# Gate projection of a SwiGLU layer as seven block products instead of eight, in a hand-scheduled decoder kernel

## The reference, cut to what matters

```python
def swiglu(x, w_up, w_down):
    gate, up = jnp.split(x @ w_up, 2, axis=-1)
    return (jax.nn.silu(gate) * up) @ w_down

for i in range(DEPTH):
    ...
    x = x + y
    x = x + swiglu(rms_norm(x, norm_ffn[i]), ffn_w_up[i], ffn_w_down[i])
    gate = jax.nn.sigmoid(x @ ple_w_gate[i] + ple_b_gate[i])
    x = x + gate * (p[i] @ ple_w_proj[i])
```

## Time and profile before

| what | value |
|---|---|
| time, median of 3 runs | 1915.02 us (1914.77 to 1915.72) |
| span of the profiled execution | 1913.6 us |
| PE busy | 1878.2 us, 98% of the span, 13698 matmuls |
| ACT, DVE, POOL busy | 729.3, 742.3, 784.1 us (38%, 39%, 41%) |
| chain that ended last | PE 86%, issue 5%, DVE 3%, POOL, ACT and DMA 2% each |
| matmuls of the shared `job` (L2292) in that chain | 72% of the span |

### The profile page before, as it was taken

The page is one execution under the profiler, slowest core; times in us unless marked ns, Lnnn a source line. Parts: engine busy times, 40 slices in busy tenths (PEclk is TensorE's granted clock), DMA queues, the critical chain, the costliest instruction groups (busy, mean ns, idle before and its releaser), DMA issues.

```text
span 1913.6 us, 35924 instructions
## 1 busy us (share of the span) xinstructions
PE 1878.2 (98%) x13698; PEld 1742.4 (91%) x13698; DVE 742.3 (39%) x871; ACT 729.3 (38%) x1091; POOL 784.1 (41%) x662
## 2 busy tenths in 40 slices
PE   7999999999999999999999999999999999999997
PEld 7999999999999999998555655999999999999997
DVE  6777632111111122697766668222231111111213
ACT  4676733322222234543433343423433322212333
POOL 3333554444554544565110110544535545544541
PEclk9999999999999999999999999999999999999999
DMA  4222232222222222423479678232322222222222
GB/s 128 91 76 84 88 96 73 82 89 83 82 83 81 82 79 77 97 72 99 146 259 312 231 253 297 89 94 70 107 78 82 83 83 82 81 85 83 78 83 78
DMA packets 187278, 210.26 MB, mean 110 GB/s; under 512 B 24483, under 2 KB 150051, under 8 KB 187119
## 3 DMA queue, kind: packets, MB, share of 16 engines
q1 hardware_dynamic: 186946, 208.71, 35.3%
q10 hardware_dynamic: 224, 0.07, 0.0%
HBM read 168.09 MB, written 40.64 MB: 109 GB/s over the span
## 4 chain that ended last, share of the span: by engine, by line
PE 86%; issue 5%; DVE 3%; POOL 2%; ACT 2%; DMA 2%; ACTq 0%; POOLq 0%; SPq 0%; DVEq 0%
PE ps L2292 72%; POOL W_LO L671 2%; PE ps L2677 2%; PE ps L2640 2%; PE ps L2579 2%; PE ps L2618 1%; DMA out_ml_C_s_dram<-C_HALVES 1%; PE ps L2513 1%; PE ps L2628 1%; PE ps L2697 1%; DVE H_PAD L1731 1%; PE ps L2502 0%; PE ps L2573 0%; PE ps L2524 0%; PE ps L2706 0%
## 5 line engine op out<-in xcount | busy, mean ns | idle before, releaser
L671 POOL TENSOR_TENSOR W_LO<-W_RAW,W_HI 128x512 fp32r<-128x512 f32 x464 | 631.1, 1369 | 717.9 <-ACT W_HI L972 651.4
L972 ACT ACTIVATE W_HI<-W_RAW 128x512 fp32r<-128x512 f32 x484 | 299.0, 628 | 709.0 <-PE ps L2292 703.8
L2292 PE MATMUL ps<-A_HI,W_HI 128*128 128x288 f32 x2296 | 493.9, 297 | 8.7 <-DVE A_LO L1567 4.8
L2292 PE MATMUL ps<-A_LO,W_HI 128*128 128x288 f32 x2296 | 492.2, 296 | 0.0
L2292 PE MATMUL ps<-A_HI,W_LO 128*128 128x288 f32 x2296 | 492.0, 296 | 0.0
L2292 PEld LDWEIGHTS ps<-A_HI,W_HI 128*128 128x128 f32 x2296 | 370.2, 189 | 11.3 <-issue 8.8
L2292 PEld LDWEIGHTS ps<-A_HI,W_LO 128*128 128x128 f32 x2296 | 370.4, 189 | 0.0
L2292 PEld LDWEIGHTS ps<-A_LO,W_HI 128*128 128x128 f32 x2296 | 370.4, 189 | 0.0
L1813 DVE TENSOR_TENSOR X<-X,ps 128x1152 f32 (+1 forms) x36 | 48.8, 1354 | 312.4 <-PE ps L2292 312.4
L2292 PE MATMUL ps<-G_HI,W_HI 128*128 128x288 f32 x768 | 164.7, 296 | 0.5 <-DVEq L1839 0.5
L2292 PE MATMUL ps<-G_HI,W_LO 128*128 128x288 f32 x768 | 164.4, 296 | 0.0
(11 more groups left out here) (404 smaller groups left out, 2254.0 us busy)
## 6 DMA issues: line engine op xcount, KB each, us to landing
W_RAW<-in_ffn_w_up_dram SPq DMA_DIRECT2D x176, 256.0 KB, 2.8
C_HALVES<-in_state_mlstm_C_dram SPq DMA_DIRECT2D x64, 512.0 KB, 5.1
out_ml_C_s_dram<-C_HALVES SPq DMA_DIRECT2D x64, 512.0 KB, 5.3
W_RAW<-in_ffn_w_down_dram SPq DMA_DIRECT2D x88, 256.0 KB, 2.6
W_RAW<-in_ml_w_in_dram SPq DMA_DIRECT2D x64, 256.0 KB, 2.8
W_RAW<-in_rg_w_in_dram SPq DMA_DIRECT2D x48, 256.0 KB, 2.8
W_RAW<-in_ple_w_gate_dram SPq DMA_DIRECT2D x32, 256.0 KB, 2.6
W_RAW<-in_ml_w_out_dram SPq DMA_DIRECT2D x32, 256.0 KB, 2.8
```

The source lines that it names most:

```text
L671: pool.tensor_tensor(W_LO[:, s], W_RAW[:, s], W_HI[:, s].bitcast(F32), ALU.subtract).then_inc(lo_ready, 1)
L972: act.activation(W_HI[:, s], W_RAW[:, s], ACT.Copy).then_inc(hi_ready, 1)
L2292: ins = pe.matmul(ps[:, 4 * s + 2 * m + h, 0:HALF_T], a[:, w, k, wc], x[:, h * HALF_T:h * HALF_T + HALF_T], start=i == 0 and k == 0 and q ...
```

## The change

A gate slab is a 2 x 2 block of weights, and the tokens it meets are a 2 x 2 block too (two input chunks, two halves). The product of two 2 x 2 blocks takes eight block products, or seven with the scheme of Winograd and Strassen, if sums and differences of blocks are made first and the seven results are combined afterwards. The change does this for every gate job but the first of each layer (`seven`), 10 of 11 in each layer, so 21 matmuls a slab in place of 24.

- **Weights.** VectorE makes four sums or differences from each pair of raw slabs (`weight_sums`): three go to the new `SUM_RAW`, one overwrites a block of `W_RAW`. ScalarE then rounds the raw slab as before and 384 columns of sums beside it. GpSimd makes the low part of the raw slab, as before, and VectorE that of the sums (`sums_lo`).
- **Tokens.** Four sums of token blocks for each pair of chunks are made once per layer (`scaled_pair` and `sums_hi` on ScalarE, `token_sums` on VectorE), beside the first gate and up jobs, and kept in `B_HI` and `B_LO` (called `T_HI`, `T_LO`), which are free then.
- **Results.** Seven banks hold the products, the eighth is spare; ScalarE copies the first product out, VectorE combines (`combine`). The up job takes the spare bank, the first product's, and two that the first step of combining frees. So TensorE waits for single steps of VectorE.
- The loops of all engines in the channel mixer are written out, and the eight DMAs that store mixer states go ahead of layer 1's mixer instead of behind the kernel's last slabs.

The diff, cut to its core:

```diff
+FORMS = {"11": (0, 0, 0), "12": (0, 1, 0), "22": (0, 1, 1), "s3": (0, 0, 1), "s1": (1, 0, 0), "s2": (1, 1, 0), "s4": (1, 2, 0)}
+PRODUCTS = [("11", "x11"), ("12", "x21"), ("s2", "t2"), ("s3", "t3"), ("s1", "t1"), ("s4", "x22"), ("22", "t4")]
+T_FORMS = ("t1", "t2", "t3", "t4")
...
+def seven(g, j):
+
+    return (g, j) != (0, 0)
...
@@ -964,6 +1028,13 @@
                     return
                 s = phase[0] % 4
                 phase[0] += 1
+                if isinstance(n, int) and n in SUM_SLABS:
+                    raw_t[s].adv()
+                    act.wait_ge(sums_ready, summed.adv() // 2 + 1)
+                    act.wait_ge(slab_used, n - 4 + 2 * RING)
+                    act.activation(W_HI[:, s], W_RAW[:, s], ACT.Copy)
+                    act.activation(SUM_HI[:, s], SUM_RAW[:, s], ACT.Copy).then_inc(hi_ready, 1)
+                    return
                 act.wait_ge(raw_loaded[s], raw_t[s].adv())
                 stand_alone(act)
...
+            def scaled_pair(i, gain):
+
+                for m in range(2):
+                    ins = act.activation(GATED[:, m, :], X[:, 2 * i + m, :], ACT.Copy, scale=VECS1[:, gain + 2 * i + m:gain + 2 * i + m + 1])
+                ins.then_inc(y_scaled, 1)
+
+            def sums_hi(layer, i):
+
+                act.wait_ge(t_raw, 4 * layer + i + 1)
+                act.activation(T_HI[:, 2 * i:2 * i + 2, :], GATE[:, :, :], ACT.Copy).then_inc(t_hi, 1)
+
+            def first_product(layer, g, j):
+
+                q = seven_number(layer, g, j)
+                act.wait_ge(product_done, 4 * q + 1)
+                act.activation(FIRST_PRODUCT[:, :], ps[:, seven_banks(g, j)[0][0], 0:HALF_T], ACT.Copy).then_inc(first_out, 1)
+
+            def ffn(layer, gain, last_out, gh):
                 for g, (g0, gn) in enumerate(GROUPS):
-                    with loop(act, gn // 2, {**split_per(8), jobs: 8, uses[0]: 1, uses[1]: 1, blk: 1}) as j:
+                    for j in range(gn // 2):
                         for k in range(4):
+                            if not seven(g, j):
+                                scaled_pair(k, gain)
+                            elif k == 3:
+                                first_product(layer, g, j)
                             split_hi()
+                            if not seven(g, j):
+                                sums_hi(layer, k)
 
                         b = blk.adv()
-                        act.wait_ge(psum_freed[0], uses[0].adv())
-                        stand_alone(act)
...
+            def token_sums(layer, i):
+
+                dve.wait_ge(y_scaled, 4 * layer + i + 1)
+                x, t = pair4(GATED[:, :, :]), pair4(GATE[:, :, :])
+                link(dve.tensor_tensor(t[:, 0:4:2], x[:, 1:4:2], x[:, 0:2], ALU.subtract))
+                link(dve.tensor_tensor(t[:, 1], x[:, 3], t[:, 0], ALU.subtract))
+                dve.tensor_tensor(t[:, 3], x[:, 2], t[:, 1], ALU.subtract).then_inc(t_raw, 1)
+                dve.wait_ge(t_hi, 4 * layer + i + 1)
+                dve.tensor_tensor(T_LO[:, 2 * i:2 * i + 2, :], GATE[:, :, :], T_HI[:, 2 * i:2 * i + 2, :].bitcast(F32),
+                                  ALU.subtract).then_inc(t_ready, 1)
+                dve.wait_ge(t_ready, 4 * layer + i + 1)
+
+            def weight_sums(layer, g, j, s):
+
+                n = seven_first(layer, g, j)
+                for k in (s, s + 1):
+                    dve.wait_ge(raw_loaded[k], 16 * (n // 4 + 1))
+                w = W_RAW[:, s:s + 2]
+                w11, w21, w12, w22 = w[:, :, 0, 0:P], w[:, :, 0, P:2 * P], w[:, :, 1, 0:P], w[:, :, 1, P:2 * P]
+                s1, s2, s4 = (SUM_RAW[:, s:s + 2, i, :] for i in range(3))
+                link(dve.tensor_tensor(s1, w21, w22, ALU.add))
+                link(dve.tensor_tensor(w21, w11, w21, ALU.subtract))
+                link(dve.tensor_tensor(s2, w22, w21, ALU.subtract))
+                dve.tensor_tensor(s4, w12, s2, ALU.subtract).then_inc(sums_ready, 1)
+
+            def sums_lo(layer, g, j, k):
+
+                dve.wait_ge(hi_ready, seven_first(layer, g, j) + k + 1)
+                dve.tensor_tensor(SUM_LO[:, k], SUM_RAW[:, k], SUM_HI[:, k].bitcast(F32), ALU.subtract).then_inc(lo_dve, 1)
+
+            def combine(layer, g, j):
+
+                q = seven_number(layer, g, j)
+                (_, p2, p6, p7, p5, p3, p4), _ = seven_banks(g, j)
+                c = pair4(GATE[:, :, :])
+                dve.wait_ge(first_out, q + 1)
+                dve.wait_ge(product_done, 4 * q + 2)
+                dve.tensor_tensor(c[:, 0:2], two_banks((p2, p6)), FIRST_PRODUCT[:, :].unsqueeze(1).broadcast_to([P, 2, HALF_T]), ALU.add)\
+                    .then_inc(combined, 1)
+                dve.wait_ge(combined, 4 * q + 1)
+                dve.wait_ge(product_done, 4 * q + 3)
+                dve.tensor_tensor(c[:, 2], ps[:, p7, 0:HALF_T], c[:, 1], ALU.add).then_inc(combined, 1)
+                dve.wait_ge(combined, 4 * q + 2)
+                dve.wait_ge(product_done, 4 * q + 4)
+                dve.tensor_tensor(c[:, 1:4:2], c[:, 1:3], ps[:, p5, 0:HALF_T].unsqueeze(1).broadcast_to([P, 2, HALF_T]), ALU.add)\
+                    .then_inc(combined, 1)
+                dve.wait_ge(combined, 4 * q + 3)
+                dve.wait_ge(slab_used, jobs.adv(4) + 2 * RING)
+                dve.tensor_tensor(c[:, 1:3], c[:, 1:3], two_banks((p3, p4)), ALU.add).then_inc(combined, 1)
+                dve.wait_ge(combined, 4 * q + 4)
+                dve.tensor_tensor(pair5(GATE[:, :, :]), pair5(GATE[:, :, :]), RB, ALU.mult).then_inc(gate_scaled, 1)
...
+            def ahead(layer, g, j, part):
+
+                if part == 0:
+                    weight_sums(layer, g, j, 0)
+                    weight_sums(layer, g, j, 2)
+                    for k in range(3):
+                        sums_lo(layer, g, j, k)
+                else:
+                    sums_lo(layer, g, j, 3)
+
             def ffn(layer, hi, lo):
                 for g, (g0, gn) in enumerate(GROUPS):
-                    with loop(dve, gn // 2, {jobs: 8, uses[0]: 1, uses[1]: 1, blk: 1, ys: 1, step: 1}) as j:
+                    ks = gn // 2
+                    for j in range(ks):
...
                         y = ys.adv()
-
-                        dve.wait_ge(slab_used, jobs.adv(4) + 2 * RING)
-                        dve.tensor_tensor(pair5(GATE[:, :, :]), psv[:, 0, :, :, 0:HALF_T], RB, ALU.mult).then_inc(psum_freed[0], 1)
-                        uses[0].adv()
+                        if seven(g, j):
+                            combine(layer, g, j)
+                        else:
+                            for i in range(4):
+                                token_sums(layer, i)
+                            dve.wait_ge(slab_used, jobs.adv(4) + 2 * RING)
+                            dve.tensor_tensor(pair5(GATE[:, :, :]), psv[:, 0, :, :, 0:HALF_T], RB, ALU.mult).then_inc(psum_freed[0], 1)
+                            uses[0].adv()
+                            if layer:
+                                dve.wait_ge(stored, 16 * 8)
+                        if j + 1 < ks:
+                            ahead(layer, g, j + 1, 0)
                         dve.wait_ge(slab_used, jobs.adv(4) + 2 * RING)
                         dve.wait_ge(silu_done, y)
                         dve.wait_ge(y_lo, b - 1 + FIRST)
-                        link(dve.tensor_tensor(pair5(GATED[:, :, :]), psv[:, 1, :, :, 0:HALF_T], pair5(GATE[:, :, :]), ALU.mult))
-                        dve.nop().then_inc(psum_freed[1], 1)
-                        uses[1].adv()
+                        if seven(g, j):
+                            q = seven_number(layer, g, j)
...
+                        if j + 1 < ks:
+                            ahead(layer, g, j + 1, 1)
+                        if seven(g, j):
+                            dve.wait_ge(up_out, 2 * q + 2)
...
+                q = seven_number(layer, g, j)
+                banks = seven_banks(g, j)[0]
+                first = j == (g == 0)
+                for i in range(4):
+                    pe.wait_ge(lo_dve, dve_slabs.adv())
+                    pe.wait_ge(lo_ready, slabs.adv() + RING)
+                    w = phase[0] % 4
+                    phase[0] += 1
+                    for p, (weight, tokens) in enumerate(PRODUCTS):
+                        if i == 0:
+                            if p == 0 and q % len(SEVEN_JOBS) == 0:
+                                pe.wait_ge(t_ready, 4 * (layer + 1))
+                            if p == 0 and first:
+                                pe.wait_ge(psum_freed[0], uses[0].now())
...
+                            elif p == 4 and first:
+                                pe.wait_ge(psum_freed[1], uses[1].now())
+                            elif p == 4 or p == 5:
+                                if not first:
+                                    pe.wait_ge(up_out, 2 * q - (p == 4))
+                        of_sums, at_k, at_m = FORMS[weight]
```

(28 more changed lines are left out.)

195 lines of the change are left out of this document (147 added, 48 removed).

## The result

The changed kernel takes 1928.2 us (median of 4 runs, 1926.6 to 1934.1) against 1915.4 before on the same chip: a ratio of 1.0068, with a 95% interval of 1.0055 to 1.0080. It is slower by 12.8 us; forecast were 1935 us and a range of 1922 to 1948.

A forecast was written before the change was run, and what follows sets the result against it. TensorE was taken to bound the kernel, 86% of the span. 1913.6 - 32.0 + 41.6 + 3.2 + 2.1 + 3.6 + 1.6 = 1933.7 us, plus 1.4 for the runs' median: 1935 us, range 1922 to 1948.

The forecast's parts named there:

- 240 matmuls fewer: Gate jobs of both layers: 10 jobs x 2 layers x 4 slabs x 3 matmuls at 133.4 ns removed, 32.0 us saved.
- ways in, with their clock term: Entry to each layer's mixer: TensorE waits 20.8 us a layer, 41.6 in both; lower clock after the pause adds 3.2.
- steady jobs: Jobs not first of their group, 14 in all: VectorE's second bank step 0.15 us late each, 2.1 us.
- group starts: First gate job of groups two and three: second banks freed 0.4 us late, four times, 1.6 us.
- turn-in: After the last up job: transposes wait for VectorE's second step, 1.8 us a layer, 3.6 us.
- rival (c): Seven products cost as much as eight if three in a row to one bank run slower: 1967 us, chance 0.03.
- four rounds: Token sums at the way in: a round takes 5.7 us against the 3.2 TensorE needs for a slab.
- exclusion: VectorE instructions with two SBUF inputs and GpSimd splits exclude each other: ways in 41.6 us with it, 24.6 without.
- Rival (a): No exclusion that matters between VectorE and GpSimd: ways in 24.6, clock 0, steady 0, 1913 us; chance 0.06.
- the wait at the 13th matmul: First seven-product job of each layer: TensorE waits for banks that the up sums free, 3.6 us lost.
- the third wait of 2.45: First up job: slab 3 starts at 322.9, 2.45 us lost to the token-sum rounds.
- Rival (b): Steady jobs starve on the shared port: each of 14 loses 1.2 us instead of 0.15, +15, 1950 us; chance 0.14.

The follow-up runs named there:

- experiment 1: Changed kernel without the token sums (plain token blocks in their place, part of the computation left out): 1888.5 us, ratio to before 0.985.
- experiment 8: Changed kernel with GpSimd splitting only 16 of 512 columns for the four slabs of each layer's first product job, behind the token-sum rounds: 1919.7 us.
- experiment 9: Changed kernel with GpSimd splitting only 16 of 512 columns for the four slabs of each layer's first up job, within the token-sum rounds: 1924.1 us.
- experiment 4: Changed kernel with 36 filler matmuls a layer in TensorE's pause ahead of the first product job: 1929.2 us, ratio to before 1.0059.
- Experiment 5: Changed kernel without VectorE's low parts of weight sums; TensorE uses the rounded sums twice, part of the computation left out: 1917.8 us.
- experiment 11: Changed kernel with TensorE's ten transposes moved ahead of its wait for the last up sums: 1923.7 us, ratio to before 1.0043.
- experiment 12: Changed kernel with early token-sum rounds, the first product job's up sums taken out earlier, and transposes ahead of the last up-sum wait: 1896.5 us.
- experiment 2: Changed kernel with the first two gate jobs of each layer plain, 9 of 11 made with seven products: 1923.7 us, ratio to before 1.0031.
- experiment 3: Changed kernel with token-sum rounds moved earlier, the first into the last job ahead of the root; one plain gate job: 1908.6 us.
- experiment 6: Changed kernel with early token-sum rounds and two plain gate jobs a layer together: 1897.1 us, ratio to before 0.9898.
- experiment 7: Changed kernel with early token-sum rounds, and the first product job's low parts two to four put behind the up sums: 1900.0 us.
- experiment 10: Kernel with early token-sum rounds and two plain gate jobs, ScalarE's first two splits of the second plain job moved ahead of the silu: 1890.0 us.

## Why the prediction was right, step by step

| term of the sum | forecast | measured |
|---|---|---|
| 240 matmuls fewer | -32.0 | -32.0, and -1.3 as a product's matmul starts 132.6 ns after the last, not 133.4 |
| ways in, with their clock term | 41.6 + 3.2 = 44.8 | 20.0 + 20.6 = 40.6 |
| steady jobs | 2.1 | 0 |
| group starts | 1.6 | 0.8 (11.33 against 11.14 us, four times) |
| turn-in | 3.6 | 1.8 + 1.4 = 3.2 |
| clock behind the turn-in | none | 1.4 |
| sum | +20.1 | +12.7 |

**The saving** is as worked out, and experiment 1 shows it unmixed. The matmuls in one bank start, if anything, a little closer than the others; rival (c) is out, as the earlier trace rows had said.

**The way in** was right in its mechanism: four rounds on VectorE in front of the gate sums, each longer than TensorE's 3.2 us, then the weight sums with an empty buffer. The round was put at 5.7 us and is 5.3. The first product job starts 34.4 us behind the start of the squares where 36.3 was forecast; that 340.2 in the forecast and 339.8 in the trace agree is luck, since the whole mixer begins 1.5 us later in that execution. That exclusion costs was argued from the earlier trace rows and is shown by experiments 8 and 9, rounds and low parts apart. The Trainium skill's page SBUF — State Buffer, "Who interferes with whom", says that two SBUF inputs of VectorE contend with GpSimd's reads; the runs agree, down to a sum that takes 0.46 us alone and 1.40 behind a split. Rival (a), which had no exclusion that matters, is out. Experiments 8 and 9 took 4.8 and 2.9 us off layer 0's way in. If these add, which no run shows, 12.3 us would be left of 20.0, and 12.3 is what the prediction had without exclusion; the short splits also save GpSimd's own time, so not all of it is VectorE's waiting.

**The mis-sized term is the clock with the wait at the 13th matmul.** The prediction added 3.6 us of wait and 1.6 us of slow matmuls a layer. They lie on one another: the first twelve matmuls ran at half clock ahead of a wait for VectorE and so cost nothing (experiment 4), the wait being 1.2 us, not 3.6. In exchange the matmuls behind it were slow, 11.45 and 12.07 us for 72 that take 9.6 at the full clock, 1.9 and 2.5. The same holds in the up job, where a slab at the lower clock (5.8 us) took the place of the third wait of 2.45. Together 20.0 and 20.6 us stand where 22.4 was forecast.

**Steady jobs** were put at 0.15 us each with a slack of nothing in the second bank step, and lose nothing. In the job that starts at 392.27 VectorE's second step is over at 393.96, and TensorE asks at 394.26: 0.3 us to spare, not 0.15 late. The third low part was done at 390.97, 22.6 us behind the start of the gate job before, where the forecast had 24.45, and VectorE then waited 1.5 us for TensorE. Experiment 5 leaves the jobs at 11.14 with the low parts taken out of VectorE. Rival (b), with 0.14 the weightiest, is out: sums and splits get in each other's way in these jobs too (a 256-column sum took 1.54 us at 385.87 instead of 0.42), but what is late has slack.

**The turn-in** has its wait, and experiment 11 takes it away. What was missing is the clock, a term that the sum did not have: behind the 1.62 us of pause and the transposes, the granted clock was 0.66 in the first 5 us of layer 1's last piece, which took 1.4 us longer. The clock fell after layer 0's turn-in as well (the first 12 matmuls of the down jobs took 2.7 us instead of 1.7). There the time to the next sum of squares was still 0.5 us shorter than before, as the matmuls that followed came 130 ns apart instead of 133; why, no run shows.

The sum was 7.4 us too high: 4.2 in the ways in and their clock, 3.4 in the steady jobs and the quicker products, 0.8 in the group starts, 0.4 in the turn-in, less 1.4 for the clock that was not forecast.

## What to carry to other kernels

An added preparation that is hidden in the steady state costs where a pipeline is entered with nothing ahead of it: price the entry by itself, and look for the engine that then works without a pause (here VectorE), since its whole queue, not the instruction named in the wait, sets how late everything is. A saving of 1.6 us in each of ten jobs was more than undone by one opening of 20 us a layer, and 38 us came back when the same instructions were put where that engine and ScalarE had been idle, with one saving job given up. Slow matmuls ahead of a wait are free and a short second pause is dear, so waits and clock are not to be added up.

## What the runs showed of the hardware

- VectorE's 288-column sum of two SBUF operands: 0.46 us alone, 1.40 beside a 512-column split of GpSimd, 0.46 beside one of 16 columns. Three low parts of 384 columns: 4.72 us beside full splits, and 0.5 to 0.6 each beside short ones.
- A pause of 1.6 us with ten transposes behind it lowers the clock sometimes, in layer 0 in seven and in layer 1 in five of the eleven profiled executions that have it. Experiments 11 and 12, in which the pause is gone, and the kernel before show no fall in either layer; with so few executions that is a sign and no proof. With that same pause in front, the last 696 matmuls took 94.4 to 94.5 us in the profiled runs of the changed kernel and of experiments 1, 2, 3 and 9, and 93.0 in those of 4, 5, 6, 7, 8 and 10. What decides it stays open.
- TensorE kept at work with idle matmuls held the full clock through the pause (139 ns each), and lost it in the next one, of 2.6 us (granted clock 0.66 from 345 to 350).
